# An encoder of two layers on one core: order of attention and of the down projection, tiles of down weights, and start

## The reference

```
h = x @ w_in                            # 1024 -> 1792, split into aq ak av bq bk bv cx
oa = chunked window attention, 6 heads of 64, 2 KV heads, a sink logit per head
ob = differential attention, 6 heads: (softmax(q1 k1) - lam * softmax(q2 k2)) @ v, chunk-causal,
     then RMS-normalized per head
oc = four pooling windows of cx, a 64x64 product per group
x = layer_norm(ALPHA * x + concat(oa, ob, oc) @ w_o)
h = x @ w_up                            # 1024 -> 2 * 2816
hc = causal convolution of 3 taps over the tokens of h, g, u = split(hc)
x = layer_norm(ALPHA * x + (silu(g) * u) @ w_down)     # 2816 -> 1024
```

## Time and profile before

| | |
|---|---|
| median of 3 runs | 2867.54 us (2866.67 to 2870.62) |
| the profiled execution | 2857.7 us |
| its span, first to last instruction | 2855.5 us |
| mean granted clock of TensorE | 0.946 |
| busy: TensorE, VectorE, ScalarE, GpSimd | 2537.2, 1498.2, 829.9, 1286.9 us |
| HBM read, written | 226.32 MB, 20.71 MB |

### The profile page before, as it was taken

The page is one execution under the profiler, slowest core; times in us unless marked ns, Lnnn a source line. Parts: engine busy times, 40 slices in busy tenths (PEclk is TensorE's granted clock), DMA queues, the critical chain, the costliest instruction groups (busy, mean ns, idle before and its releaser), DMA issues.

```text
span 2855.5 us, 30205 instructions
## 1 busy us (share of the span) xinstructions
PE 2537.2 (89%) x11608; PEld 2028.2 (71%) x11608; DVE 1498.2 (52%) x2845; ACT 829.9 (29%) x1709; POOL 1286.9 (45%) x724
## 2 busy tenths in 40 slices
PE   5987897999988998999999989988888879899996
PEld 3765676777766777777777777766666767788885
DVE  4245536565555377246665377144455563656545
ACT  1032313444432122035453122033344421222211
POOL 3521243334334555564444545542343335566663
PEclk7997898999999999999999999999999999999998
DMA  4622322223222222442322223431222213233332
GB/s 129 200 83 59 92 74 74 78 74 85 83 69 60 81 81 68 132 119 83 100 76 67 81 74 96 120 91 55 75 78 82 60 45 96 89 96 115 105 90 74
DMA packets 336065, 249.01 MB, mean 87 GB/s; under 512 B 37358, under 2 KB 306994, under 8 KB 335922
## 3 DMA queue, kind: packets, MB, share of 16 engines
q1 hardware_dynamic: 310384, 210.99, 25.1%
q10 hardware_dynamic: 25538, 36.09, 4.8%
HBM read 226.32 MB, written 20.71 MB: 87 GB/s over the span
## 4 chain that ended last, share of the span: by engine, by line
PE 68%; DVE 17%; ACT 5%; issue 3%; DMA 2%; ACTq 2%; POOL 2%; SPq 0%; DVEq 0%
PE psum L709 40%; PE psum L933 13%; PE psum L803 5%; PE psum L739 3%; PE psum L760 2%; PE psum L791 2%; DVE conv L1299 2%; DVE conv L1302 2%; DVE room L1194 2%; ACT conv L1123 2%; POOL w_lo L687 1%; ACTq L969 1%; DMA w_raw<-in_w_o 1%; DVE room L1218 1%; DVE mid L1458 1%
## 5 line engine op out<-in xcount | busy, mean ns | idle before, releaser
L685 POOL CAST w_hi<-w_raw 128x1024 fp32r<-128x1024 f32 x360 | 404.4, 1123 | 1499.6 <-DMA w_raw<-in_w_up 849.6
L687 POOL TENSOR_TENSOR w_lo<-w_raw,w_hi 128x1024 fp32r<-128x1024 f32 x360 | 887.5, 2465 | 28.9
L709 PE MATMUL psum<-x_hi,w_hi 128*128 128x512 f32 x2048 | 855.6, 418 | 43.2 <-POOL w_lo L687 21.9
L709 PE MATMUL psum<-x_hi,w_lo 128*128 128x512 f32 x2048 | 820.0, 400 | 0.0
L709 PE MATMUL psum<-x_lo,w_hi 128*128 128x512 f32 x2048 | 819.2, 400 | 0.0
L709 PEld LDWEIGHTS psum<-x_hi,w_hi 128*128 128x128 f32 x2048 | 398.9, 195 | 136.3 <-POOL w_lo L687 29.0
L933 PE MATMUL psum<-hid,w_hi 128*128 128x512 f32 x1408 | 458.4, 407 | 11.9 <-DVE x_res L1501 11.7
L709 PEld LDWEIGHTS psum<-x_hi,w_lo 128*128 128x128 f32 x2048 | 396.6, 194 | 88.6
L709 PEld LDWEIGHTS psum<-x_lo,w_hi 128*128 128x128 f32 x2048 | 399.0, 195 | 75.0 <-issue 2.5
L1299 DVE SCALAR_TENSOR_TENSOR conv<-psum,prm_all,conv 128x511 f32<-128x511 f32 x176 | 131.7, 748 | 413.4 <-ACT conv L1123 413.3
L933 PEld LDWEIGHTS psum<-hid,w_hi 128*128 128x128 f32 x1408 | 264.4, 195 | 68.2 <-DVE x_res L1501 15.8
(11 more groups left out here) (126 smaller groups left out, 2379.1 us busy)
## 6 DMA issues: line engine op xcount, KB each, us to landing
w_raw<-in_w_up SPq DMA_DIRECT2D x176, 512.0 KB, 4.0
w_raw<-in_w_down SPq DMA_DIRECT2D x88, 512.0 KB, 3.5
w_raw<-in_w_in SPq DMA_DIRECT2D x36, 512.0 KB, 3.9
w_raw<-in_w_o SPq DMA_DIRECT2D x32, 512.0 KB, 4.0
qk_scratch<-stage_qk SPq DMA_DIRECT2D x48, 256.0 KB, 3.4
q_stack<-qk_scratch ACTq DMA_DIRECT2D x72, 128.0 KB, 2.7
k_stack<-qk_scratch ACTq DMA_DIRECT2D x36, 256.0 KB, 4.8
w_raw<-in_w_in SPq DMA_DIRECT2D x16, 384.0 KB, 3.4
```

Of the source, the lines that this page charges most:

```text
L685: nc.gpsimd.tensor_copy(w_hi[:, slot, :], w_raw[:, slot, :]).then_inc(s["w_high"], 1)
L687: nc.gpsimd.tensor_tensor(w_lo[:, slot, :], w_raw[:, slot, :], w_hi[:, slot, :].bitcast(F32), ALU.subtract).then_inc(s["w_ready"], 1)
L709: mm = nc.tensor.matmul(o, w, v[:, k, :], start=(k == 0 and w is wh and v is x_hi[h]), stop=(k == KT - 1 and w is wl))
```

## The change

- `LAG` goes. In both halves AT comes two steps after A1, before AW, and AV at the end of the same step. AV writes its own bank (the upper half of `tb`) with semaphores of its own, `pv` and `o_read`; AT waits for the former AV's reader only where it is wider than that half. The buffer of the exponentials is laid out anew (`e_of`): four units of two maps in half 0, three units of the first map and one second map in half 1.
- Two down events follow each up tile from the sixth on; the rest come last, behind `UE`. A tile of down weights holds 512 outputs for both hidden tiles of a pair, instead of 1024 outputs for one.
- On VectorE the taps of a gate tile come before the product of the former pair.
- Some shares of the planner change.
- ScalarE issues its small loads after the copies of the first four x tiles, both layers' parameters in one load each (9 loads are counted by `small`, 10 by `stage_in`); VectorE's part moves to the event `PR`. The first weight tile is loaded behind two x tiles.

The diff, cut to its core:

```
 def attend(l, h):
-    lag = LAG[h]
     out = [("AS", l, h)] * ((l, h) == (0, 1)) + [("AL", l, h)]
-    for u in range(UNITS + lag + 1):
+    for u in range(UNITS + 2):
         if u < UNITS:
             out.append(("A1", l, h, u))
-        if u > lag:
-            out.append(("AV", l, h, u - lag - 1))
+        if u >= 2:
+            out.append(("AT", l, h, u - 2))
         if 1 <= u <= UNITS:
             out.append(("AW", l, h, u - 1))
         if u < UNITS and h == 1 and unit_of(u)[0] == "b":
             out.append(("A2", l, h, u))
-        if lag <= u < UNITS + lag:
-            out.append(("AT", l, h, u - lag))
+        if u >= 2:
+            out.append(("AV", l, h, u - 2))
     return out

 def feed_forward(l, h):
-    def up(g):
-        return [("U", l, h, 2 * g + j, v, part) for j in range(2) for v in range(2) for part in range(PARTS)]
-    def down(g):
-        return [("D", l, h, g, d) for d in range(KT)]
-    out = [("H", l)] * h + up(0)
-    for g in range(1, GROUPS):
-        out += up(g)
-        if g == GROUPS - 1:
-            out.append(("UE", l, h))
-        out += down(g - 1)
-    return out + down(GROUPS - 1)
+    downs = [("D", l, h, g, d) for g in range(GROUPS) for d in range(KT)]
+    out = [("H", l)] * h
+    for n in range(2 * FT):
+        out += [("U", l, h, n // 2, n % 2, part) for part in range(PARTS)]
+        if n >= 5:
+            out += downs[2 * (n - 5):2 * (n - 4)]
+    return out + [("UE", l, h)] + downs[2 * (2 * FT - 5):]

 def share(e):
     if kind in ("A1", "A2", "AW"):
         wide = width_of(e[2], e[3])[1] / HALF
-        return 0.3 + 0.6 * wide * (2 if ... else 1) + 4.0 * (e[3:] == (0,) and kind == "A1")
+        return 0.4 + 0.6 * wide * both + 4.0 * (kind == "A1" and e[3] == 0)
     if kind == "P":
-        return 4.0 if e[3] == "c0" else 0.5
+        return 5.0 if e[3] == "c0" else 0.5
     if kind == "LO":
-        return 3.0 if e[4] == 0 else 2.5
+        return 6.0 if e[4] == 0 else 2.5
     if kind == "O":
-        return 3.0 if e[3] == 0 else 0.5
-    return {"AV": 0.4, "AT": 0.6, "V": 0.5, "MR": 2.0, "M": 3.0, ...
+        return 4.0 if e[3] == 0 else 0.5
+    if kind == "M":
+        return 7.0 if e[3] == 0 else 2.0
+    return {"AV": 0.6, "AT": 0.6, "V": 0.5, "MR": 2.0, ...

+        def e_of(h, u, m, width):
+            at = (u % 4 * 2 + m) * HALF if h == 0 else (u % 3 if m == 0 else 3) * S
+            return e_buf[h][:, at:at + width]

 SyncE
-                    sp.dma_start(slot, w_down_v[l, :, 2 * tile[3] + tile[5], :]).then_inc(done, 16)
+                    c = tile[4] * P
+                    sp.dma_start(slot.rearrange("p (j c) -> p j c", j=2),
+                                 w_down_v[l, :, 2 * tile[3]:2 * tile[3] + 2, c:c + HALF]).then_inc(done, 16)
...
+            for t in range(HT):
+                sp.dma_start(x_in[0][:, t, :], x_rows[t]).then_inc(x_landed[t], 16)
+                if t == 1:
+                    fill(0)
+                    filled[0] = 1
             fill_free(None)
+            sp.dma_start(ratio, pool_ratio.rearrange("p (c t) -> p c t", c=2)).then_inc(s["ratio_in"], 16)

 TensorE
             def weights_turned(e):
                 pe.wait_ge(s["weights"], after(("AW", l, h, u), "weights"))
                 take(e)
+                if u >= 1 and width_of(h, u)[1] > HALF:
+                    pe.wait_ge(s["o_read"], after(("AV", l, h, u - 1), "o_read"))
...
             def sums(e):
-                take(e)
+                pe.wait_ge(s["tb_free"], after(("AT", l, h, u), "tb_free"))
+                if u >= 1:
+                    pe.wait_ge(s["o_read"], after(("AV", l, h, u - 1), "o_read"))
                 for b in range(width // P):
-                    mm = nc.tensor.matmul(wide("tb")[:, 0:HD], ...
+                    mm = nc.tensor.matmul(wide("tb")[:, HALF:HALF + HD], ...
-                mm.then_inc(s["tb_full"], 1)
+                mm.then_inc(s["pv"], 1)
...
                 elif kind == "D":
                     if d == 0:
                         made = ("U", l, h, 2 * g + 2, 1, PARTS - 1) if g + 1 < GROUPS else ("UE", l, h)
                         pe.wait_ge(s["hid_low"], after(made, "hid_low"))
-                        for j in range(2):
-                            tile_in(e[:4] + (0, j))
+                    if d % 4 == 0:
+                        tile_in(e)
                     take(e)
+                    n = SLOT[e[:4] + (d // 4 * 4,)]
                     for j in range(2):
-                        n = SLOT[e[:4] + (0, j)]
-                        wh, wl = (w[:, n, d * P:(d + 1) * P] for w in (w_hi, w_lo))
+                        c = j * HALF + d % 4 * P
+                        wh, wl = (w[:, n, c:c + P] for w in (w_hi, w_lo))

 ScalarE
+            def constants():
...
                 elif kind == "X":
...
+                    if (h, i) == (0, HT - 1):
+                        constants()

 VectorE
                     if kind_e == "A2":
+                        if u >= 1:
+                            dve.wait_ge(s["weights"], after(("AW", l, h, u - 1), "weights"))
                         logits_of(e, u, 1, o, True)
...
                 elif kind == "PR":
+                    constants()
                     dve.wait_ge(s["tb_full"], after(e, "tb_full"))
...
                 elif kind == "U":
+                    taps(e)
                     if v == 0 and f > 0:
                         product(l, h, f - 1)
-                    taps(e)
                     if v == 1 and f > 0:
                         low_hidden(h, f - 1, before(e, "hid_high"))
```

More of the change, by code:

```diff
@@ L52 @@
 PARTS = 4
-LAG = (2, 1)
 TAP = [0, 44, 128]
@@ L141, in share @@
         wide = width_of(e[2], e[3])[1] / HALF
[L142 removed]
+        both = 2 if kind == "A1" and e[2] == 0 and unit_of(e[3])[0] == "b" else 1
+        return 0.4 + 0.6 * wide * both + 4.0 * (kind == "A1" and e[3] == 0)
     if kind == "P":
[L144 removed]
+        return 5.0 if e[3] == "c0" else 0.5
     if kind == "LO":
[L146 removed]
+        return 6.0 if e[4] == 0 else 2.5
     if kind == "O":
[L148 to L149 removed]
+        return 4.0 if e[3] == 0 else 0.5
+    if kind == "M":
+        return 7.0 if e[3] == 0 else 2.0
+    return {"AV": 0.6, "AT": 0.6, "V": 0.5, "MR": 2.0, "LM": 2.0, "LE": 2.0, "LF": 1.5}.get(kind, 1.0)
 def length(e):
@@ L225, in ring_of @@
         return "sb"
-    if kind in ("AT", "AV"):
+    if kind == "AT":
         return "tb"
@@ L297, in signals @@
     if kind == "AV":
-        return {"tb_full": 1, "tb_free": 1}
+        return {"pv": 1, "o_read": 1}
     if kind == "MR":
@@ L382, in tiles_of @@
         return [e]
-    if e[0] == "D" and e[4] == 0:
-        return [e + (j,) for j in range(2)]
+    if e[0] == "D" and e[4] % 4 == 0:
+        return [e]
     return []
@@ L393, in ends @@
     if kind == "D":
-        return tile[:4] + (KT - 1,), "d_full"
+        return tile[:4] + (tile[4] + 3,), "d_full"
     if kind == "V":
@@ L627, in _ @@
             sp.dma_start(ident, identity[:, :]).then_inc(s["ident_in"], 16)
-            for t in range(HT):
-                sp.dma_start(x_in[0][:, t, :], x_rows[t]).then_inc(x_landed[t], 16)
             filled = [0]
@@ L953, in _ @@
                 for at, g, src in rows:
-                    act.dma_start(stage[at:at + src.shape[0], l, g, :], src).then_inc(s["stage_in"], 16)
+                    act.dma_start(stage[at:at + src.shape[0], :, g, :], src).then_inc(s["stage_in"], 16)
                 for h in range(2):
-                    act.dma_start(stage[90:91, l, 1, HD * h:HD * (h + 1)],
-                                  b_subln_g[l].rearrange("(a c) -> a c", a=1)).then_inc(s["stage_in"], 16)
-            act.dma_start(ratio, pool_ratio.rearrange("p (c t) -> p c t", c=2)).then_inc(s["small"], 16)
@@ L959, in _ @@
-            act.dma_start(m_a, mask_a[:, :]).then_inc(s["small"], 16)
-            act.dma_start(m_b, mask_b[:, :]).then_inc(s["small"], 16)
+                    act.dma_start(stage[90:91, :, 1, HD * h:HD * (h + 1)],
+                                  b_subln_g.rearrange("(a l) c -> a l c", a=1)).then_inc(s["stage_in"], 16)
+                act.dma_start(m_a, mask_a[:, :]).then_inc(s["small"], 16)
+                act.dma_start(m_b, mask_b[:, :]).then_inc(s["small"], 16)
             def load_head(h, head):
@@ L1191, in logits_of @@
                         dve.wait_ge(s["ta_landed"], after(at, "ta_landed"))
-                dst, bias = e_buf[h][:, u % (2 * LAG[h]), m, 0:width], bias_table(l, h, u, width)
+                dst, bias = e_of(h, u, m, width), bias_table(l, h, u, width)
                 if kind == "b":
@@ L1246, in roots @@
             def roots(l, h):
-                dve.wait_ge(s["tb_free"], after(("AV", l, h, UNITS - 1), "tb_free"))
+                dve.wait_ge(s["o_read"], after(("AV", l, h, UNITS - 1), "o_read"))
                 o = o_tok[h][:, :, A_W:]
@@ L1328, in low_hidden, with constants @@
                     .then_inc(s["hid_low"], 1)
```

(15 more changed lines are left out.)

58 lines of the change are left out of this document (28 added, 30 removed).

## The result

The changed kernel takes **3057.99 us** (median; 3044.73 to 3074.28), the kernel before 2867.54 beside it: 1.067 times as long, interval 1.0636 to 1.0706. Both are medians of five executions, and those of the kernel before lie between 2860.00 and 2870.99. I had predicted 2876, 2820 to 2930. The sign of my forecast was right, its size was not: 190 us slower instead of 8. The profiled execution took 3074.28 us, its span is 3072.4 (before 2857.7 and 2855.5).

What follows compares the result with a forecast made beforehand. The prediction took TensorE to bound the kernel, losing time to idle waits and a lower clock. Its terms, 158 + 33 - 120 - 48 - 15 = +8 us on 2867.5, gave 2876 us, range 2820 to 2930 (8 in 10).

Steps and rivals of the forecast that it cites:

- What bounds it: Whole kernel: everything waits for TensorE, and each idle us loses about 0.4 us more to the lower clock.
- Down tiles in pairs: Feed-forwards: each group's first down event newly waits for VectorE's low_hidden; +158 us with clock, bounds 100 and 210.
- a sign of being wrong: Third joint stage: TensorE's idle time still above 90 us would show the prediction wrong.
- The lock: Rival, feed-forwards: each low part meets GpSimd at its worst, 1.9 us more, forty times; +75, 2951 us; chance 0.04.
- First half: First half's attention: the sum, now in its transpose's step, waits for ScalarE's copy; +33 us with clock, bounds 0 and +80.
- the copy behind the exponentials: Rival, first half's attention: the sum's wait for the copy costs in every unit, +80 instead of +33; 2923 us; chance 0.07.
- Lag of two in the second half: Second half's attention: later transposes and the sums' own bank remove 86 idle us; -120 us with clock, bounds -70 and -150.
- Down tiles by halves: Down weight loads: one tile for four outputs, same bytes in rows half as long, costs 0.
- Shares: Normalization and attention output turns: larger planner shares, with VectorE's spread additions, shorten waits; -48 us with clock, bounds -20 and -65.
- The start: Kernel start: x tiles come first, so the first projection starts earlier; -15 us, bounds -5 and -22.
- The mixed stages hide the new wait: Rival, first three joint stages: waiting at first down events lets attention work catch up; -52, 2824 us; chance 0.30.
- Nothing hides it: Rival, all joint stages: the down events' wait is uncovered and the clock falls each time; 202, 2920 us; chance 0.13.

Runs made afterwards that it cites:

- e5: The changed kernel with feed-forward groups by turns again (four up tiles, eight down events) and the first half's sum a step later: 2695.07 us, 0.9409 of the kernel before.
- e3: The changed kernel with the down pairs one up tile later and the first half's sum AV one step later: 2738.18 us, 0.9561 of the kernel before.
- e4: The changed kernel with the feed_forward of the kernel before, groups of four up tiles and eight down events by turns: 2822.32 us, 0.9855 of the kernel before.
- e1: The changed kernel with only the down pairs moved one up tile later: 2860.53 us, 0.9979 of the kernel before.
- e2: The changed kernel with only the first half's sum AV one step later again: 2947.11 us, 1.0296 of the kernel before.
- e8: The kernel before with only the down events in pairs and the tiles of down weights by halves: 3006.74 us, 1.0504 of the kernel before.
- e9: The changed kernel with the first half's transposes ahead of the step's scores, sums in the same step: 3010.31 us, 1.0476 of the kernel before.
- e11: The changed kernel with feed-forward groups by turns and the first half's transposes ahead of the scores, sums in the same step: 2752.18 us, 0.9597 of the kernel before.
- e6: e5 with the planner's shares of the kernel before: 2736.25 us, 0.9554 of the kernel before.
- e10: The kernel before with only the new start of the change: 2854.49 us, 0.9956 of the kernel before.

## Why the prediction was wrong

**What bounds it: right, with a factor too small.** In every run TensorE works off the same 11608 matmuls, so the span is its idle time and a busy time that grows as its clock falls. I put 0.4 us of clock beside each idle us. My own rows gave rather 0.48: 91 us at half speed lose 45 us, beside 94.9 idle. Idle and busy time of TensorE (the windows over whole spans, busy as shown, idle as the rest):

| kernel | idle, us | busy, us |
|---|---|---|
| e5 | 206.0 | 2487.5 |
| e3 | 236.2 | 2496.3 |
| e4 | 274.3 | 2541.5 |
| e1 | 304.7 | 2559.7 |
| before | 318.3 | 2537.2 |
| e2 | 373.1 | 2567.9 |
| e8 | 408.9 | 2589.3 |
| e9 | 414.9 | 2593.3 |
| after | 440.8 | 2631.6 |

From e5 to after busy time rises by 144.1 us over 234.8 idle, 0.61 for each; from before to after it is 94.5 over 122.5, 0.77. Kernels that differ mainly in one of the two waits tell them apart. The wait ahead of the down events (e3 to e2, e1 to after, e4 to after, before to e8) brings 137, 136, 167 and 91 us of idle time and 72, 72, 90 and 52 of busy time: 0.52 to 0.58 for each idle us. The wait ahead of the first half's sums (e5 to e4, e3 to e1, e2 to after) brings 68 us of idle time each time and 54, 63 and 64 of busy time: 0.79 to 0.94. So the sums' short waits (129.2 us in 71 waits) cost more clock for each idle us than the longer ones ahead of the down events (192.1 us in 44); why is not shown. The changed kernel has 4 us at a mean clock of 0.50 behind the wait at 2695.61, with TensorE busy throughout:

```profile
2696.00:2700.00 4.00, 4.00 (x10) 3.07 (x10) 0.69 (x1) 0.00 (x0) 3.18 (x2) 0.50 0.00 0
```

**Down tiles in pairs: the mechanism right, +158 was +236.** This is one of the two steps that failed. The wait stands where I put it, and the last stage's idle time came out as priced, 43.6 us for the ten groups and the final one, against 41 and 1 (a quarter of the four for the final groups):

```profile
L946 PE MATMUL psum<-hid,w_hi 128*128 128x512 f32 x352 | 123.7, 436 | 43.6 <-DVE hid L1343 43.6
```

In part that was luck. Eight of the ten waits are 3.5 to 4.2 us long, on average below my 4.1, one is 5.1, and one, 8.30 us, makes up for them: even in this stage a normalization stands in front once. The stage has 22.9 us more busy time (386.58 against 363.69 in the earlier trace rows) where I had 14. The first three stages did not come out. 192.1 - 43.6 = 148.5 us stood ahead of their 33 groups; I had 78 and 3. The sentences that failed are those that costed a mixed group as the bare chain of 3.3 or 3.7 us less what attention hides. I took the chain from one stretch that had nothing else on VectorE, and asked only what hides it, not what lengthens it. Group by group, 27 of the 33 cost 2.1 to 5.5 us, 3.3 on average against my 2.6, so attention hid less than I took off; six cost 7.2 to 12.9, 58 us together against 16. In the three of these that I followed, VectorE stood in a normalization, in the attention output's, or in splits of x ahead of low_hidden.

The clock was the other part of this miss. The profiled runs of e4 and of the changed kernel differ by 257 us (their medians by 236): 167 of them are idle time, where I had 123, and 90 are busy time, where I had 35. I had let the clock fall at eight of the last stage's gaps and at two in five of the others. The idle time of the third stage, for which I had named 90 us as a sign of being wrong, is 89.8 us: what attention saved there, these waits took.

**The lock, in a place where I had not looked.** I gave it a chance of 0.04, for low_hidden meeting GpSimd. There it did little: L1343 is 931 ns on average in the last stage, where I had taken 1.09 us. But in the 12.87 us wait it shows twice: L436 on 128x4 elements takes 2.20 us, from 1800.94 to 1803.14, beside GpSimd's L694, 1800.77 to 1803.12; in the next row the same line takes 0.16. L1474 takes 2.19 us and ends at 1807.47, L694 at 1807.45. That is 4.1 of the 12.87 us. (A third such row there, L436 again, takes 0.89 us and ends 0.02 us after GpSimd's L692.) The last stage's 8.30 us wait has the same:

```profile
2731.35 2.35 POOL L694 TENSOR_TENSOR w_lo<-w_raw,w_hi 128x1024 fp32r<-128x1024 f32 x1
...
2731.53 2.20 DVE L436 TENSOR_TENSOR lst<-lst 128x4 f32<-128x4 f32 x1
```

The Trainium skill, "SBUF — State Buffer", section "SBUF: two separate sides", says that such a pair exclude each other for a whole instruction. By that rule the tiny instructions of a normalization can each cost as much as GpSimd's long one, and the trace agrees. No run took GpSimd's work away to measure the sum of it.

**First half, +33 was +111 to +127.** The second step that failed. I had the copy behind the exponentials as a rival at +80, with a chance of 0.07, and spoke against it with the 5.5 us of the earlier trace rows. That row belongs to the old order, in which the sum came a step after its transposes; it says nothing of a sum in the same step. "58% of a step covers that" did not hold: beside the feed-forward the sums wait 48.6 us, not 11.5 (5.5 and my 6), and in layer 0 62.0, not 31. Here too the clock came on top: the later sum takes 68 us of idle time away and 54 to 64 of busy time, where I had 24 and 10. e9 and e11 show that the wait goes when the transposes and the copy come ahead of the exponentials, and that most of it then stands at the transposes: two steps seem too few for the way of a unit, wherever the copy lies.

**Lag of two in the second half, -120: the total right, its parts not.** From the kernel before to e6 it is -132 us; e6 has the lag, the own bank, the new start, the new tiles of weights and VectorE's taps first, but the old groups and shares and, in the first half, sums as late as before. Less the start's 13, 119 are left for all of this. By the profiled runs they are 63 us of idle and 49 us of busy time, where I had 86 and 34. The transposes' wait did fall, over both halves from 94.9 to 11.3 us. But the sums' rose from 48.1 to 59.8 and the scores' (L760, L774 in e6), which I had expected to go in the second half, from 12.7 to 28.1, so attention's three waits together fell by 56 us, both halves counted. Another 20 us come from the wait for GpSimd's `w_lo`, 23.4 before and 2.9 in e6, which I had not priced. That all this met my -120 was luck in part.

**Down tiles by halves: 0.** The same -119 holds them, and e8 them and the pairs. Nothing shows a cost. In every kernel that has them the wait for `w_lo` is shorter than before, 2.5 us in e5, 2.7 in e4 and 7.2 in e8 against 23.4, so they may well be a gain that I did not price; but no run had them alone.

**Shares, -48: right.** 35 of it were for the shares, -41 measured (e6); the other 13 were for VectorE's spread additions, whose wait fell from 11.7 to 2.0 us in the changed kernel and whose gain is inside the 236. **The start, -15: -13 measured (e10), right;** TensorE's first projection starts at 19.24 instead of 38.57, where I had 17.

The terms with their measured sizes: 236 + 127 - 119 - 41 - 13 = +190, which is 3058. (The five are differences of medians of different kernels along one path, from before over e6, e5 and e4 to after, so that they close; only the start was also run by itself.) My error of 182 us is 78 in the first, 94 in the second, 10 in the rest. Both steps failed toward the cheap side, and in the same two ways: a wait of the new order was priced from a quiet row of the old order, and too little clock was put beside it.

**The rivals.** "The mixed stages hide the new wait", to which I gave 0.30, was wrong: cover there was less than what VectorE's other work added. "Nothing hides it" had the right side, 202, and was still too small. e8 shows that the first one has some truth where the old waits are still there, 97 us of it.

## What to carry to other kernels

Before an instruction is moved to where another engine's product is only just made, list everything that stands ahead of that product on its engine at each such place, not only at the quietest one, and take the lengths from the trace with their maxima. Lengthen a pipeline of several engines by whole steps, and count the steps along the whole way: a link moved forward inside its step hands the wait to the link before it. A lag is right for one stage and wrong for another, so try it by stage: two steps did for the second half, three for the first, and the best kernel (groups by turns, e5) took those and left the pairs.

## What was not expected of the hardware

An instruction of VectorE on 128x4 elements can take 2.20 us instead of 0.16, beside a GpSimd tensor_tensor of 2.35 us. And waits are not alike in what they do to TensorE's clock: for each idle us TensorE was busy 0.52 to 0.58 us longer with the waits ahead of the down events, 4.4 us long on average, and 0.79 to 0.94 us longer with the first half's waits ahead of the sums; over the whole run the sums' waits are 1.8 us long on average.
